# A two-layer recurrent decoder on one core: the mixers' projections and gates in three rounded products

## What is computed

```python
u = x @ p['w_in'][l] + p['b_in'][l]
(rw, mqk, mv, mo, mi, mf, gq, gk, gv, gg, ga, rx, ry, gates) = _split(u, IN_SIZES)
...
branches = jnp.stack([o_a, o_b, o_c, o_d], axis=2)
up = jnp.einsum('blgc,gcd->blgd', branches, p['w_branch'][l])
gate = jax.nn.sigmoid(gates.reshape(B, L, N_BRANCH, D))
merged = jnp.einsum('blgd,blgd->bld', gate, up)
out = merged @ p['w_out'][l]
...
x = _layer_norm(DN_ALPHA * x + m_out, p['ln1_g'][l], p['ln1_b'][l])
f = _swiglu(...) if l % 2 == 0 else _moe(...)
x = _layer_norm(DN_ALPHA * x + f, p['ln2_g'][l], p['ln2_b'][l])
```

## Time and profile before

| | |
|---|---|
| time, median of 3 (range) | 1970.82 us (1970.04 to 1975.36) |
| the profiled execution's time / its span | 1969.92 us / 1968.1 us |
| mean granted TensorE clock | 0.963 of full speed |
| busy: PE / DVE / ACT / POOL | 94% / 64% / 42% / 1% |
| mixer of layer 0 in the trace | 9.4 to about 404 us |
| its output projection starts | 371.92 us |

### The profile page before, as it was taken

How to read it: one execution, slowest core, us unless ns; L and a number is a source line. 1 busy time by engine, 2 the same in 40 slices (tenths; PEclk the granted TensorE clock), 3 DMA queues, 4 the chain that set the end, 5 groups by cost and what they waited for, 6 DMA issues and landing times.

```text
span 1968.1 us, 24319 instructions
## 1 busy us (share of the span) xinstructions
PE 1852.4 (94%) x9310; PEld 1517.5 (77%) x9310; DVE 1255.4 (64%) x1507; ACT 834.0 (42%) x856; POOL 15.3 (1%) x32
## 2 busy tenths in 40 slices
PE   8999999979998999999995999999899999999896
PEld 6777788879997867778874877777687877777685
DVE  2656634146643436753326887889798978888794
ACT  1222112133332312311103666666666656766673
POOL 1000000000001000000000000000000000000000
PEclk9999999989998979999995999999999999999999
DMA  8330222535553423311214897988798988989770
GB/s 345 120 103 19 119 108 77 181 129 174 191 192 101 135 70 106 124 68 51 109 49 186 306 351 272 338 323 336 276 342 319 342 300 317 344 319 343 278 299 22
DMA packets 59290, 402.71 MB, mean 205 GB/s; under 512 B 8672, under 2 KB 9344, under 8 KB 11312
## 3 DMA queue, kind: packets, MB, share of 16 engines
q1 hardware_dynamic: 54144, 393.80, 53.8%
q0 software_dynamic: 1600, 3.97, 0.6%
q10 hardware_dynamic: 3440, 3.41, 0.5%
HBM read 396.67 MB, written 4.49 MB: 204 GB/s over the span
## 4 chain that ended last, share of the span: by engine, by line
PE 50%; DVE 2%; ACT 2%; issue 2%; DVEq 0%; ACTq 0%
PE mA L1813 30%; PE mW L1813 19%; ACT WH L642 1%; PE mA L1742 1%; ACT X L917 0%; DVE HEL L1091 0%; DVE ring_low L969 0%; DVE V L1611 0%; DVE XEL L1059 0%; PE mW L1695 0%; DVE SQ L1613 0%; DVE SQ L1605 0%; DVE XTL L976 0%; PE mW L1714 0%; ACT V L910 0%
## 5 line engine op out<-in xcount | busy, mean ns | idle before, releaser
L969 DVE TENSOR_TENSOR ring_low<-ring,WH 128x2048 fp32r<-128x2048 f32 x192 | 438.4, 2290 | 82.5 <-ACT WH L642 81.3
L1813 PE MATMUL mA<-X,ring 128*128 128x264 f32 x1664 | 397.0, 393 | 17.7 <-DMA ring<-in_w_in_dram 9.4
L642 ACT ACTIVATE WH<-ring 128x2048 fp32r<-128x2048 f32 x188 | 359.1, 1913 | 66.7 <-PE mW L1813 56.2
L1813 PEld LDWEIGHTS mA<-X,ring 128*128 128x128 f32 x1664 | 316.5, 193 | 80.6 <-issue 17.0
L1813 PE MATMUL mA<-WH,XEH 128*128 128x512 f32 x704 | 295.0, 419 | 9.0 <-DVE XEL L1059 7.6
L1813 PE MATMUL mA<-WH,XEL 128*128 128x512 f32 x704 | 279.7, 397 | 0.0
L1813 PE MATMUL mA<-ring_low,XEH 128*128 128x512 f32 x544 | 216.7, 398 | 0.0
L969 DVE TENSOR_TENSOR more_low<-more_ring,WH 128x2048 fp32r<-128x2048 f32 x72 | 164.9, 2290 | 23.3 <-ACT WH L642 23.0
L1813 PEld LDWEIGHTS mA<-WH,XEH 128*128 128x128 f32 x704 | 134.2, 191 | 40.5 <-DVE ring_low L969 11.3
L1813 PEld LDWEIGHTS mA<-WH,XEL 128*128 128x128 f32 x704 | 134.0, 190 | 31.7
L642 ACT ACTIVATE WH<-more_ring 128x2048 fp32r<-128x2048 f32 x72 | 137.7, 1912 | 24.5 <-PE mW L1813 21.0
(11 more groups left out here) (386 smaller groups left out, 2809.7 us busy)
## 6 DMA issues: line engine op xcount, KB each, us to landing
ring<-in_moe_dram SPq DMA_DIRECT2D x192, 1024.0 KB, 4.8
more_ring<-in_moe_dram SPq DMA_DIRECT2D x72, 1024.0 KB, 4.9
ring<-in_w_in_dram SPq DMA_DIRECT2D x52, 1024.0 KB, 6.2
ring<-in_ffn_up_dram SPq DMA_DIRECT2D x20, 1024.0 KB, 4.8
ring<-in_ffn_down_dram SPq DMA_DIRECT2D x11, 1024.0 KB, 4.8
ring<-in_w_branch_dram SPq DMA_DIRECT2D x7, 1024.0 KB, 5.0
RTAIL<-in_w_in_dram SPq DMA_DIRECT2D x6, 1024.0 KB, 5.3
ring<-in_w_out_dram SPq DMA_DIRECT2D x6, 1024.0 KB, 9.1
```

What stands on the lines that cost most here:

```text
L642: nact.activation(WH[:, HI_SLOT[j % PAIR], :], expert_slot(j), ACT.Copy).then_inc(weights_hi, 1)
L969: v.tensor_tensor(expert_low(j), expert_slot(j), WH[:, HI_SLOT[j % PAIR], :].bitcast(F32), SUB)\
L1813: return nc.tensor.matmul(out, w, x, start=start, stop=stop, skip_group_check=True)
```

## The change

- The first two pairs of a layer (PLAIN) stay float32 matmuls. For the other 27 PE issues three fp32r matmuls for each: 54 tiles of 24.
- Per layer ACT gets 54 roundings of half a pair (128x1024) and DVE 54 subtractions of half a pair, out of their `streamed()` generators; before layer 0's first pair, and after each LN2 of layer 0, x is rounded and subtracted in two halves.
- Raw weights lie in a ring of four slots, where DVE overwrites them with their remainders. The rounded copies alternate between two other slots (HI_SLOTS), and early in a layer two more lie where MG and GT come later. HI_AHEAD says how many pairs before its use a pair is rounded: two for the first 14, one for the rest.
- `w_branch` has one slot (UP_SLOT). The up tiles of a branch come one gate pair later than before, those of RWKV at the end.
- In the FFN the remainders also go in place, there are four rounded copies, not two, and a slot is freed by PE. Its first two remainders are made during the output projection.
- The constant for the means is one column read 128 times over.
- The three tables get other numbers. PE_FILL's sum goes from 449 to 1315, ACT_FILL's from 50 to 109, DVE_FILL's from 32 to 86.

```diff
-SLOTS = 9
-MSLOTS = 8
+SLOTS = 7
+MSLOTS = 9
...
+def streamed_work():
+    seq = [("u", i) for i in (TMI - 1, TRX, TRY, TMQ, TMK, TMV, TMO, TGQ, TGV, TGG, TR, TK, TV)]
+    late = []
+    for g in (RG, ML, GL, RW):
+        for q in range(4):
+            seq.append(("gate", g, q))
+            late.append(("up", g, q))
+            if len(late) > 1 and late[0][1] != RW:
+                seq.append(late.pop(0))
+    return seq + late
+STREAM = streamed_work()
+PAIRS = [item for item in STREAM if item[0] != "up"]
+PLAIN = 2
+HI_PLACE = [0, 1, "mg", "gt", 0, 1, "mg", "gt", 0, 1, "gt", "mg"] + [0, 1] * 8
+HI_AHEAD = [2] * 14 + [1] * 13
+RAW = ((0, 1, 2, 3), (3, 4, 5, 6))
+HI_SLOTS = ((4, 5), (0, 1))
+UP_SLOT = (6, 2)
+FF_SLOTS = (4, 5, 6, 0, 1, 2, 3)
...
+PE_FILL = {"loads9": 25, "rg.conv": 95, "ml.qk": 228, "ml.logd0": 16, "ml.kw3": 9, "ml.abs": 7, "ml.h": 44,
...
+        slots_rounded = sb("slots_rounded", [P, SLOTS, SLOT], F32R, at=where["slots"])
+        mg_rounded = sb("mg_rounded", [P, SLOT], F32R, at=where["BIG"] + 4 * (NU + GR) * T)
+        gt_rounded = sb("gt_rounded", [P, SLOT], F32R, at=where["BIG"] + 4 * NU * T)
+        HH, HL = sb("HH", [P, FT, T], F32R, at=where["BIG"]), sb("HL", [P, FT, T], F32R)
+        FWH = sb("FWH", [P, 4, SLOT], F32R)
...
+        weights, last_user, landings, splits = [], {}, [0] * SLOTS, [0]
+        class Weight:
+            def __init__(self, source, slot, user, place=None):
+                self.source, self.slot, self.user = source, slot, user
+                self.freed = last_user.get(slot)
+                last_user[slot] = user
+                landings[slot] += 1
+                self.landed = slot_in[slot], 16 * landings[slot]
+                self.raw, self.low = slots[:, slot, :], slots_rounded[:, slot, :]
+                if place is not None:
+                    self.rounded, key = place
+                    self.place_freed = last_user.get(key)
+                    last_user[key] = user
+                    self.split = splits[0]
+                    splits[0] += 1
+                weights.append(self)
+            def hi(self, half):
+                return hi_done, 2 * self.split + half + 1
+            def lo(self, half):
+                return lo_done, 2 * self.split + half + 1
...
+        for l in range(DEPTH):
+            for n, item in enumerate(PAIRS):
+                if item[0] == "u":
+                    source, user = A["w_in"][l, item[1] // 2], pe_of.at("u.tile", l, 2 * n + 1)
+                else:
+                    _, g, q = item
+                    source, user = A["w_in"][l, NU // 2 + 4 * g + q], pe_of.at("gate.tile", l, 2 * n + 1 - NU)
+                place = hi_place(l, n - PLAIN) if n >= PLAIN else None
+                of_pair[l, n] = Weight(source, RAW[l][n % 4], user, place)
+                if item in (PAIRS[NU // 2 - 1], ("gate", ML, 3), ("gate", GL, 3), ("gate", RW, 3)):
+                    g = item[1] if item[0] == "gate" else RG
+                    ups = KT * (RG, ML, GL, RW).index(g)
+                    of_up[l, g] = Weight(A["w_branch"][l, g], UP_SLOT[l], pe_of.at("mg.up", l, ups + KT - 1))
+            for p in range(4):
+                of_out[l, p] = Weight(A["w_out"][l, p], RAW[l][(len(PAIRS) + p) % 4], pe_of.at("mg.out", l, 2 * p + 1))
+            if l == 0:
+                for i in range(2 * FC + 12):
...
+            for i, w in enumerate(weights):
+                if w.freed:
+                    sp.wait_ge(*w.freed)
+                sp.dma_start(w.raw, w.source).then_inc(slot_in[w.slot], 16)
...
+            def round_x(half):
+                tiles = slice(4 * half, 4 * half + 4)
+                nact.activation(XH[:, tiles, :], X[:, tiles, :], ACT.Copy).then_inc(x_hi, 1)
+            act.wait_ge(x_in, 16)
+            for half in range(2):
+                round_x(half)
...
+                    for n, item in enumerate(PAIRS):
+                        while split < len(PAIRS) - PLAIN and split + PLAIN <= n + HI_AHEAD[split]:
+                            w = of_pair[l, PLAIN + split]
+                            act.wait_ge(*w.landed)
+                            if w.place_freed:
+                                act.wait_ge(*w.place_freed)
+                            for half in range(2):
+                                nact.activation(halves_of(w.rounded, half), halves_of(w.raw, half), ACT.Copy).then_inc(hi_done, 1)
+                                yield
+                            split += 1
...
                     act.wait_ge(*dve_of.at("rw.branch", l))
-                    round_ffn(0)
-                    round_ffn(1)
+                    for i in range(3):
+                        round_ffn(i)
...
-                    if item[0] not in ("merge", "up"):
+                    if item[0] != "up":
+                        n += 1
+                        if PLAIN <= n < len(PAIRS):
+                            w = of_pair[l, n]
+                            for half in range(2):
+                                dve.wait_ge(*w.hi(half))
+                                v.tensor_tensor(halves_of(w.low, half), halves_of(w.raw, half),
+                                                halves_of(w.rounded, half).bitcast(F32), SUB).then_inc(lo_done, 1)
+                                yield
...
+            def split_tile(kind, l, i, w, q, name):
+                free(numbers[kind, l, i])
+                wh, wl = (x.rearrange("p (k n) -> p k n", k=KT)[:, :, P * q:P * q + P] for x in (w.rounded, w.low))
+                for k in range(KT):
+                    if q == 0 and k % 4 == 0:
+                        pe.wait_ge(*w.lo(k // 4))
+                    for a, x in ((wh, XH), (wh, XL), (wl, XH)):
+                        ins = mm(acc(kind, l, i), a[:, k, :], x[:, k, :], k == 0 and a is wh and x is XH, k == KT - 1 and a is wl)
+                        if k == KT - 1 and a is wl:
+                            ins.then_inc(*pe_of.step(name, i))
+                        yield
...
+                        if item[0] != "up":
+                            w = of_pair[l, n]
+                            kind, i0 = ("u", 2 * n) if item[0] == "u" else ("gate", 2 * n - NU)
+                            if n < PLAIN:
+                                yield from plain_pair(kind, f"{kind}.tile", l, i0, w, xs)
+                            else:
+                                if n == PLAIN:
+                                    pe.wait_ge(x_lo, 4 * l + 2)
+                                for q in range(2):
+                                    yield from split_tile(kind, l, i0 + q, w, q, f"{kind}.tile")
+                            n += 1
                             continue
-                        kind, g, q2 = item
-                        if q2 == 0 and kind != "gate":
...
+                        _, g, q2 = item
+                        w = of_up[l, g]
+                        if q2 == 0:
+                            pe.wait_ge(*w.landed)
                             pe.wait_ge(*dve_of.at({RG: "rg.out", ML: "ml.branch", GL: "gl.branch", RW: "rw.branch"}[g], l))
+                        wb = w.raw.rearrange("p (k n) -> p k n", k=2)
+                        for q in range(2):
+                            f = P * (2 * q2 + q)
+                            yield from tile("up", l, up, [wb[:, k, f:f + P] for k in range(2)],
+                                            [BRANCH[g][:, k, :] for k in range(2)], "mg.up")
+                            up += 1
```

More of the change, by code:

```diff
@@ L125, in _const_cols @@
     at = 0
-    for name, n in (("ident", P), ("mean", P), ("ones", TP), ("tri", P), ("iota", P), ("iota8", NE), ("eps", 1),
+    for name, n in (("ident", P), ("mean", 1), ("ones", TP), ("tri", P), ("iota", P), ("eps", 1),
                     ("bo", P), ("bom", P), ("mb", 256), ("mk", 256), ("ml16", P), ("mlo", P),
@@ L150, in constants @@
     put("eps", np.full((P, 1), 4 * LN_EPS))
-    put("mean", np.full((P, P), 1.0 / D))
+    put("mean", np.full((P, 1), 1.0 / D))
     put("mb", np.concatenate([-1.0 * (b16 & (s < t)), -1.0 * (b64 & (s <= t))], 1))
@@ L164, in constants @@
     put("iota", np.tile(np.arange(P), (P, 1)))
-    put("iota8", np.tile(np.arange(NE), (P, 1)))
     return c
@@ L227 @@
     ("rw.p4", 2), ("rw.p8", 2), ("rw.et", 2), ("rw.wt", 2), ("n0.sq", 1),
[L228 to L229 removed]
+    ("n0.sqrt", 1), ("ln.sq", 4), ("ln.sqrt", 2), ("ln.half", 2),
+    ("ln.norm", 2), ("ff.tanh", 11),
 )
@@ L321, in program @@
         places = sb("places", [P, 576])
+        assert end[0] <= where["SCR"] + 4 * 12416
+        ring = sb("ring", [P, MSLOTS, SLOT], at=where["XH"])
+        assert end[0] <= where["con"]
         HEH, HEL = sb("HEH", [P, 2, 256], F32R, at=where["V8"]), sb("HEL", [P, 2, 256], F32R)
@@ new lines, in hi_place, with ffn_used @@
+        def hi_place(l, s):
+            p = HI_PLACE[s]
+            if p == "mg":
+                return mg_rounded[:, :], ("mg", l)
+            if p == "gt":
+                return gt_rounded[:, :], ("gt", l)
```

(18 more changed lines are left out.)

183 lines of the change are left out of this document (72 added, 111 removed), and 8 rows, old and new, of the table PE_FILL.

## The result

The changed kernel takes 1961.24 us, median of 16 (1957.09 to 1966.65), against 1974.93 us for the kernel before, median of 16 on the same chips (1970.04 to 1982.51): a ratio of 0.9938, interval 0.9923 to 0.9952. By the ratio that is 12 us less (13.7 between the medians) where I had forecast 25. The profiled execution took 1960.3 us, its span is 1958.5.

What follows compares the result with a forecast made beforehand. The prediction took PE, busy 94% of the span, as the bound, with chain and filling balanced at the mixers' seams. Terms +2.5 + 2 - 20.0 + 3 = -12.5 us a layer, -25 for both, gave 1945 us, range 1915 to 1966.

Steps and rivals of the forecast that it cites:

- What a tile costs: On PE, three fp32r matmuls (0.357 us) replace one float32 (0.445 us): at most 76 us saved for both layers.
- Term 3: From RWKV's last variance to the output projection: float32 gate filling ends last by 20 us; -20.0 us a layer.
- Term 1: Up to mLSTM's transposes: six half subtractions join DVE's chain, PE waits about 16 us for it; +2.5 us a layer.
- Terms 2 and 4: mLSTM, GLA and RWKV up to the last variance, net +2 us; lower clock after two new waits, +3 us a layer.
- the -9.7: RWKV steps -3.5 and -3.1 us, mLSTM -1.6, others -1.5, where filling ended last and gets shorter.
- The clock: Two new long PE waits, each costing up to 1.7 us of slower matmuls behind it: +3 us a layer.
- term 2: mLSTM, GLA, RWKV: places ending later +11.5 us, places ending earlier -9.7, net +2 us a layer.
- Cost at nothing: ACT's roundings mostly hidden; start, loads, FFN, experts and one-column mean taken to add no time.
- D: Rival: seven more waits with low clock, +12 us a layer, eat nearly the whole saving; 1955 to 1968, chance 0.23.
- C: Rival: subtractions on DVE's chains, mLSTM to RWKV, make it slower from 59% on the path; 2024 at worst, chance 0.10.
- B: Rival: PE stays the bound everywhere, so nearly all 76 us come; about 1895, chance 0.12.

Runs made afterwards that it cites:

- before_no_tail: The kernel before, with seven of eight matmuls of each gate tile behind RWKV's last variance left out; 2799.29 us (wrong gates changed the routing).
- thin_sub: The changed kernel with DVE's half subtractions in the mixers cut from 1024 to 8 columns; 1942.94 us, ratio 0.9859 to the kernel before.
- plain_678: The changed kernel with pairs 6 to 8 of each layer back as float32 matmuls, without rounding or subtraction; 1941.71 us, ratio 0.9828 to the kernel before.
- early_sub: The changed kernel with one half subtraction a layer (second of pair 8) moved in DVE's order ahead of mLSTM's convolution; 1955.84 us, ratio 0.9913.
- skip_xl: The changed kernel without the product of rounded weights and x's remainder in the mixers' u and gate tiles; 1957.96 us, ratio 0.9918.
- thin_skip: The changed kernel with the cuts of thin_sub and skip_xl together; 1933.77 us, ratio 0.9795 to the kernel before.
- thin_both: thin_sub with ACT's half roundings in the mixers cut to 8 columns as well; 1947.67 us, ratio 0.9864 to the kernel before.
- plain_678_20: plain_678 with pair 20 (gates of GLA) as float32 matmuls too; 1948.37 us, ratio 0.9865 to the kernel before.
- ahead: plain_678 with pair 9 float32 too, everything up to GLA's operands drawn one pair earlier, and filling between mLSTM's heads; 1940.76 us, ratio 0.9838.
- heads_gl: The changed kernel with 36 units of filling moved from gl.ops to ahead of mLSTM's heads 1 to 3; 1958.84 us, ratio 0.9917.

## Why the prediction was half right

**What a tile costs: right.** The fp32r filling runs at 0.12 us a matmul where the clock is full (starts at 88.15, 88.27, 88.39 in the changed kernel) and at 0.22 where it is low (80.59, 80.81, 81.03). Of the 76 us as the most that can come, PE's busy time gave up 47; 18 more were eaten by lower clock.

**Term 3, the tail: right.** -19.6 us a layer against -20.0; 17.95 us against 17.5. before_no_tail gives 18 of it in the kernel before.

**Term 1: direction right, +3.8 us on average with the -0.7 ahead of it, against +2.5.** The chain grew about as reckoned (up to the transposes thin_sub and plain_678 give 4 and 6.6 us back). What I missed are 1.7 us: PE waits not for the chain but for a remainder that stands in it, and then finishes its filling at the lower clock. That the last remainder before the transposes is made late in DVE's order could be read from the order; I did not ask what PE still had to do behind it. early_sub shows the size, up to the transposes.

**Terms 2 and 4: here the forecast failed.** I had +2 and +3, together +5 a layer; measured from the transposes to the last variance is +14.1 in layer 0 and +6.2 in layer 1, 10.2 on average. The failed step is the -9.7, "earlier, where filling ended last and is now shorter". The last variance, which I had put at 338 to 343 us, came at 351.72. The places where I expected the chain or the filling to end later came: from mLSTM's numerators to RWKV's first group +15.1 in layer 0 and +11.8 in layer 1, against +11.5. Of the places that were to come earlier, RWKV's group steps gave 4.4 and 3.1 us, not 6.6, and mLSTM's and the small ones nothing. The runs say this in its place. In mLSTM's part chain and filling both end near last, and taking from either alone gives nothing in layer 1 (thin_sub, skip_xl, thin_skip), so shorter filling could not pay there. From GLA's transposes on PE waits 6.2 us more than before, 1.7 of which go with the subtractions (thin_sub); the other 4.5 are a chain that the shorter filling no longer covers. With the filling a third shorter the subtractions cost 4.4 and 4.6 us there (thin_skip against skip_xl). I had treated DVE's free half of that stretch as cover. My reading is that it is free only where it waits for others, and that a subtraction put ahead of a chain step that is ready delays it. How the 5.5 us divide between subtractions, uncovered chain and clock stays open: what thin_sub gave by the clock, up to 3.4 us, did not come in thin_both.

**The clock** was mis-sized at the place of my first new wait. From the transposes to the numerators, where it is low in both kernels, it made +3.5 us in layer 0 and -2.5 in layer 1, with the same program; on average +0.5 where I had +3. So this term hid a part of the miss: without it term 2 misses by 7.7.

**Cost at nothing: right for ACT (thin_both; half a pair took 1.05 us to round, not 0.96), the FFN, the loads; wrong for the experts.** They took 3.6 us more in a program that is the same but for where its slots lie, most of it by two waits for DVE's gating product that the kernel before does not have:

```profile
1294.86 0.44 PE L1837 MATMUL mA<-con,V 128*128 128x128 f32 x2 [1.78 <-DVE V L1189]
```

The other is 1.92 us, at 1513.28. These or a wait of 2.3 us for a remainder in the second one's place stand in all variants at 927.7 to 928.5 us (plain_678_20 has the latter alone and takes 928.2), but not in plain_678 (924.9), which has the same layout in memory, and hardly in ahead (925.6). So it is not the layout, nor the 1.7 us shorter norm in front (skip_xl lacks that and has 928.1). Ahead of the wait ACT stands idle 2.6 us for nothing that the profile names. What it waits for stays open.

**The rivals.** D (1955 to 1968, chance 0.23) names the size, and much of the mechanism: more waits and more low clock. Another part is C's, subtractions on the path, in a share well below its 59%. B was wrong: skip_xl shows that a third less PE work hardly moves the total.

## What to carry to other kernels

- Filling that becomes cheaper pays where it ends last by a clear margin (here the 20 us of the tail). At seams where chain and filling were fitted to each other, count little for shorter filling, and price what the cheaper form puts into the chain, even on an engine that is half idle.
- A cheaper form need not be used everywhere. Three of 27 pairs put back to the dearer one, where their helpers stood in the chain and PE waited, made the kernel 20 us faster, more than the change itself; about 8 of it can be laid to them, the rest came with the clock and in the experts.
- When a producer's output is consumed by filling, look at its place in the producer's order, not only at its time: moving one subtraction brought the transposes 1.7 us forward. Then read on to the next seams, since a part of such a gain can go again as lower clock (here 1.0 and 1.5 us of the 1.7).
- Read both layers. The same program in layer 1 gave another answer than layer 0 for thin_sub, skip_xl, early_sub and plain_678.

## What the runs showed of the hardware

- PE at 100% busy on small matmuls with short moving operands can run at the 1.2 GHz level throughout (granted clock 0.50 in 90.80:112.70 of the changed kernel). In the heads of one program the mean granted clock was 1.00 in layer 0 and 0.57 in layer 1 (ahead), or 0.56 in layer 0 and 1.00 in layer 1 (heads_gl), and the stretch took 14.9 and 24.2 us, 28.0 and 17.1.
- The same wait of 2.72 us was followed by a granted clock of 1.00 in thin_sub and 0.88 in thin_both over the next steps. A stretch compared between two runs needs its clock beside it.
- A POOL operation of two inputs and 1024 columns takes 2.3 to 2.9 us and stretches each DVE operation beside it from 0.44 or 0.71 to 2.5 to 2.8 us.
